# Two pairs of squared tiles added on GpSimd before TensorE's norm sum, at the first two FFN entries

## The chip, the cores and the metric

The kernel runs on one core of a Trainium2 chip. The metric is the device time of one execution in microseconds (us). Engines: PE is TensorE's matmul, PEld its weight load, DVE is VectorE, ACT is ScalarE, POOL is GpSimd, SP is SyncE, which here issues transfers (DMAs).

## The reference, cut to what matters

An encoder step of two layers runs over 576 tokens (512 of a prompt and 64 of a stream), each a row of 1024 numbers in float32. Every layer has two SwiGLU FFNs around a mixer, each behind an RMS norm, so there are four FFNs in all (a, b, c and d in the kernel).

```python
def _rmsnorm(x, g):
    x32 = x.astype(jnp.float32)
    y = x32 * lax.rsqrt(jnp.mean(x32 * x32, axis=-1, keepdims=True) + EPS) * g.astype(jnp.float32)
    return y.astype(x.dtype)

def _swiglu(u, w_in, w_out):
    h = u @ w_in
    a, b = h[..., :D_FF], h[..., D_FF:]
    return (jax.nn.silu(a) * b) @ w_out
...
        x = x + 0.5 * _swiglu(_rmsnorm(x, norm_ffn1[i]), ffn1_w_in[i], ffn1_w_out[i])
```

The part at issue is the mean over the 1024 channels of x squared, for each token, at the entry of the first FFN (a) and of the second (b).

## The kernel before, in words

The activations x lie in on-chip memory with the channel on the partition: 8 tiles (j = 0 to 7) of 128 channels by 576 tokens. Two neighbouring tiles make a block kp (0 to 3). Tokens are worked in two halves of 288.

**The matmuls.** Every product is in float32 accuracy by three matmuls on a split of both operands into a high part (copied by ACT) and a low part (subtracted by DVE). For the weights, ACT copies `w_hi` (L715) and DVE subtracts `w_lo` (L1213). The input product of an FFN takes, for each pair n of hidden tiles, seven block products M1 to M7 in place of eight (Strassen's way, in Winograd's form). The moving operand is one of seven combinations of the x blocks, held in `u7`: parts 0 and 1 are single blocks and simple differences, part 2 holds the last three sums (`sums_odd`, L1255 to L1259, three DVE operations that depend on each other; the high part is copied by ACT at L757, the low part subtracted by DVE at L1267). The weights are summed likewise: SP loads raw blocks (raw_x, raw_y, raw_a), DVE adds raw_y and raw_x into raw_z (L1219), and GpSimd issues accumulating transfers onto raw_x, raw_y and raw_z (`add_s1` L569, `add_s3` L577, `add_s4` L584).

**The order of the work** is written out by hand for each engine, and every engine goes through its own list in order; semaphores tie the lists together. A ring of weight places and the reuse of the raw buffers set how early a copy or a transfer may go: SP's load of M4's weights for pair n (`load_a22`, L449) waits until `w_lo` of M4 of the pair before is made, and what SP has behind it waits with it. At a and b the products of the first pairs come in the order COLD: M1 of pairs 0 and 1, M5, M2, then M6 of pairs 0 and 1 together, block by block (kp = 0 to 3), then M7, M7, M4, M3, M1 of pair 2, M5 of pair 2, M4 of pair 1, M6 of pair 2 and so on. Each kp of the M6 group waits for `u7_made[2]`, part 2 of u of that block. M5 of pair 2 waits for `gate_second` of pair 0 (DVE, L1314), and M6 of pair 2 for ACT's copy of M1 of pair 2 (`s1_copied`, L793).

**The norm.** The products use x without its norm; the factor `rstd` of each token is applied afterwards by DVE. At a and b ACT squares each tile of x into `sq8` (`square_tile`, L761), and PE sums over the channels by a matmul of `sq8` with a matrix filled with 1/1024 (`norm_tiles`, L1867 to L1876; the matmul is L1874), two halves for each tile, accumulated over the 8 tiles. In a, 2 tiles come ahead of the M6 group and 2, 1, 1 and 2 behind its four kp steps; in b, 4 come within the first M1 group and one behind each kp step of M6. Then ACT takes the root (L766) and DVE the reciprocal in four parts (L1284). At the other norms GpSimd squares and adds tile by tile (`square`, L540 to L556: L548 squares, L551 adds).

**GpSimd's list** at the entry of a or b (`add_rest`, L586): add_s1 of pair 2, add_s4 of pair 0, add_s4 of pair 1, add_s1 of pair 3 (which waits for SP's load into raw_x), then add_s3, add_s4 and add_s1 in turn.

Of the kernel before, what the change touches and what calls it, by code (L numbers as in the profile page):

```python
# [5 lines left out]
DT = D_MODEL // P  # L6
KP = DT // 2
SEQ, DEC_SEQ = 512, 64
TOK = SEQ + DEC_SEQ
HALF = TOK // 2  # L10
# [124 lines left out]
def encoder_step(nc, a):  # L135
    F32, F32R = mybir.dt.float32, mybir.dt.float32r
    ALU, ACT = mybir.AluOpType, mybir.ActivationFunctionType
# [10 lines left out]
    def sb(name, shape, dt=F32, at=None):  # L148
        size = 4
        for s in shape[1:]:  # L150
            size *= s
        return nc.alloc_sbuf_tensor_at(name, shape, dt, offset=region(size) if at is None else at)
# [43 lines left out]
    mean_w = sb("mean_w", [P, P])  # L196
# [50 lines left out]
    sq8 = sb("sq8", [P, DT, TOK], at=sq8_at)  # L247
# [6 lines left out]
    ps = nc.alloc_psum_tensor("ps", [P, 8, 512], F32)  # L254
# [25 lines left out]
    sem = nc.alloc_semaphore  # L280
# [16 lines left out]
    sums_made = [sem("sums_even_made"), sem("sums_odd_made")]  # L297
# [5 lines left out]
    h_hi_ready, h_ready = sem("h_hi_ready"), sem("h_ready")  # L303
    sq_step, sumsq_ready = sem("sq_step"), sem("sumsq_ready")
    sq_last, sumsq_full, sq8_made = sem("sq_last"), sem("sumsq_full"), sem("sq8_made")
    mix_squared, mix_added = sem("mix_squared"), sem("mix_added")
    hist_psum, hist_root, hist_rms = sem("hist_psum"), sem("hist_root"), sem("hist_rms")
    norm_psum, norm_root, rstd_ready = sem("norm_psum"), sem("norm_root"), sem("rstd_ready")
# [13 lines left out]
    ffn_a = Ffn(0, 0, a["ffn1_in"][0], a["ffn1_out"][0])  # L322
    ffn_b = Ffn(1, 2, a["ffn2_in"][0], a["ffn2_out"][0])
# [89 lines left out]
    with block as block:  # L413
# [111 lines left out]
        def _(pool):  # L525
# [39 lines left out]
            def add_s1(f, ph, n):  # L565

                g = f.pair(ph, n)
                pool.wait_ge(a21_landed[g % 2], 16 * (g // 2 + 1))
                pool.dma_start(raw_x[g % 2][:, :], f.w_in[ph * PAIRS + n, 3, :, :], accum_op=ALU.add) \  # L569
                    .then_inc(s1_summed[g % 2], 16)  # L570
# [9 lines left out]
            def add_s4(f, ph, n):  # L580

                g = f.pair(ph, n)
                pool.wait_ge(lo_split, f.unit(ph, "M6", n) + 1)
                pool.dma_start(raw_z[g % 2][:, :], f.w_in[ph * PAIRS + n, 1, :, :], accum_op=ALU.add) \  # L584
                    .then_inc(s4_summed[g % 2], 16)

            def add_rest(f, ph):

                if order_of(f.i, ph) is COLD:
                    add_s1(f, ph, 2)  # L590
                    add_s4(f, ph, 0)
                else:
                    add_s4(f, ph, 0)
                    add_s1(f, ph, 2)
                add_s4(f, ph, 1)
                add_s1(f, ph, 3)
                for n in range(2, PAIRS):
                    add_s3(f, ph, n)
                    add_s4(f, ph, n)
                    if n + 2 < PAIRS:  # L600
                        add_s1(f, ph, n + 2)
# [67 lines left out]
        def _(act):  # L669
# [78 lines left out]
            def u7_high(f, kp, part):  # L748

                if part == 1:  # L750
                    act.activation(u7[:, kp, 0, 2:4, :], halves(x[:, 2 * kp + 1, :]), ACT.Copy,
                                   scale=ngains[:, f.norm, 2 * kp + 1:2 * kp + 2]).then_inc(u7_hi[1], 1)
                    return
                act.wait_ge(sums_made[part // 2], KP * f.i + kp + 1)
                first, end = PARTS[part]
                src = stage(f, kp)[:, first:end, :] if part else even_stage(f, kp)
                act.activation(u7[:, kp, 0, first:end, :], src, ACT.Copy) \  # L757
                    .then_inc(u7_hi[part], 1)

            def square_tile(j):  # L760
                act.activation(sq8[:, j, :], x[:, j, :], ACT.Square).then_inc(sq8_made, 1)  # L761
# [160 lines left out]
            u7_high(ffn_a, 2, 2)  # L922
            square_tile(1)
            square_tile(3)
            u7_high(ffn_a, 3, 2)
            square_tile(5)
            square_tile(7)
            ffn_in(ffn_a, 0, copied=2)
            ffn_out(ffn_a, 0)
            ffn_in(ffn_a, 1)  # L930
# [138 lines left out]
            for j in range(DT):  # L1069
# [5 lines left out]
                elif middle:  # L1075
# [3 lines left out]
                    for h in range(HEADS):  # L1079
                        last = act.activation(junk[0:L, :], v_one[0:L, c, h, 0:DV], ACT.Square,  # L1080
                                              accum_out=ssum[0:L, c, h:h + 1])
# [727 lines left out]
        def _(pe):  # L1809
# [55 lines left out]
                                   start=True, stop=True)  # L1865
                mm.then_inc(norm_psum, 1)

            def norm_tiles(f, turns):

                for i in turns:  # L1870
                    j = (0, 2, 4, 6, 1, 3, 5, 7)[i] if f is ffn_a else i
                    pe.wait_ge(sq8_made, DT * f.i + i + 1)
                    for h in range(2):
                        mm = pe.matmul(ps[:, 6 + h, 0:HALF], mean_w[:, :], sq8[:, j, h * HALF:(h + 1) * HALF],  # L1874
                                       start=i == 0, stop=i == DT - 1, skip_group_check=True)
                    if i == DT - 1:  # L1876
                        mm.then_inc(norm_psum, 1)

            def ffn_in(f, ph):
                order = order_of(f.i, ph)  # L1880
                groups = [order[t:t + 1] for t in range(len(order))]
                if order is COLD:
                    groups = [order[0:2], order[2:3], order[3:4], order[4:6], order[6:8]] + groups[8:]
                elif ph == 0:
                    groups = [order[0:4]] + groups[4:]
                needs = {"M1": 0, "M5": 0, "M2": 1, "M3": 1, "M6": 2, "M7": 2, "M4": 2}
                seen, t = set(), 0
                for products in groups:
                    if ph == 0 and t == ROOT_AT[f.i]:
                        if f is ffn_a:  # L1890
                            norm_tiles(f, range(2))
                        elif f is not ffn_b:
                            norm(f.norm)
                    t += len(products)
                    for prod, n in products:
                        product_waits(f, ph, prod, n)
                    part = needs[products[0][0]]
                    for kp in range(KP):
                        if ph == 0 and part not in seen:
                            pe.wait_ge(u7_made[part], KP * f.i + kp + 1)  # L1900
                        for prod, n in products:
                            product_mm(f, ph, prod, n, kp)
                        if order is COLD and products[0] == ("M6", 0):
                            norm_tiles(f, ((2, 3), (4,), (5,), (6, 7))[kp] if f is ffn_a else (4 + kp,))
                        elif f is ffn_b and ph == 0 and products[0] == ("M1", 0) and kp == 1:
                            pe.wait_ge(x_ready, 2 * DT + 6)
                            norm_tiles(f, range(4))
                    seen.add(part)

            def ffn_out(f, ph, tiles=DT):  # L1910
# [162 lines left out]
            for k in range(DT):  # L2073
# [4 lines left out]
                mm = block_mm(U_M + 1, k, u_tile(k), 2, k == 0, k == DT - 1)  # L2078
# [262 lines left out]
```

## Time and profile before

| | us |
|---|---|
| median of 3 runs | 1898.39 |
| lowest and highest | 1894.95, 1899.76 |
| the profiled execution, its whole time | 1898.26 |
| its span in the trace | 1896.5 |
| PE busy | 1872.6 (99%) |
| DVE busy | 1253.8 (66%) |
| ACT busy | 866.4 (46%) |
| GpSimd busy | 329.1 (17%) |

All rows are of one profiled execution, with times from the start of its span. A row of a timeline gives the start, the length, the engine, the line of the kernel, the operation, what it writes and reads, and in brackets the idle time of the engine before it with what ended it. Matmuls overlap, so the spacing of their starts tells their cost, not their length. An instruction of DVE or ACT starts some 0.09 us before the one ahead of it is shown to end.

### The profile page before, as it was taken

How to read it: one execution, taken by the hardware profiler on the slowest of the kernel's cores; microseconds unless marked ns; L12 is line 12 of the kernel's file. 1: busy time of each engine (PE TensorE's matmuls, PEld its weight loads, DVE VectorE, ACT ScalarE, POOL GpSimd, SP SyncE). 2: the span in 40 equal slices, each digit the busy share in tenths (PEclk: the TensorE clock that was granted, in tenths of full speed). 3: DMA queues.
4: the chain of work that ended last, by engine and by line, in shares of the span. 5: the costliest groups of instructions: out<-in, count | busy, mean ns of one | idle time of the engine just before them, and what ended most of it. 6: DMA issues, size and time to landing. Idle time of an engine off the chain costs nothing.

```text
span 1896.5 us, 34433 instructions
## 1 busy us (share of the span) xinstructions
PE 1872.6 (99%) x13850; PEld 1849.8 (98%) x13850; DVE 1253.8 (66%) x1998; ACT 866.4 (46%) x1516; POOL 329.1 (17%) x352
## 2 busy tenths in 40 slices
PE   8999999999999999999999999999999999999998
PEld 7999999998999999999999999999989999999998
DVE  8874487668874488678853886453446888448843
ACT  7652355346552355345532553232334665235532
POOL 2210122121220122132201221300010322012112
PEclk9999999999999999999999999999999999999999
DMA  8763576334763576347644763221113576357632
GB/s 213 163 153 92 133 168 140 106 91 91 160 145 108 122 165 148 110 98 170 145 131 101 172 138 101 84 101 67 57 45 107 116 174 143 105 121 167 129 94 79
DMA packets 116830, 234.71 MB, mean 124 GB/s; under 512 B 13184, under 2 KB 15248, under 8 KB 116672
## 3 DMA queue, kind: packets, MB, share of 16 engines
q1 hardware_dynamic: 77440, 160.59, 28.0%
q0 software_dynamic: 38208, 69.42, 22.3%
q8 instruction: 111, 1.82, 0.4%
q10 hardware_dynamic: 1024, 2.49, 0.4%
q14 instruction: 47, 0.39, 0.1%
HBM read 228.92 MB, written 3.53 MB: 123 GB/s over the span
## 4 chain that ended last, share of the span: by engine, by line
PE 90%; DVE 4%; ACT 2%; DMA 2%; issue 1%; POOL 0%; DVEq 0%; ACTq 0%; POOLq 0%
PE ps L1829 48%; PE ps L1819 39%; DVE w_lo L1213 1%; DMA raw_y<-in_ffn_in 1%; DVE u L1267 1%; PE ps L2143 1%; PE ps L2209 0%; DMA raw_z<-in_ffn_in 0%; ACT w_hi L715 0%; PE ps L2146 0%; PE ps L2011 0%; PE ps L2133 0%; DMA x<-in_x 0%; PE ps L2118 0%; DVE rstd L1284 0%
## 5 line engine op out<-in xcount | busy, mean ns | idle before, releaser
L1829 PE MATMUL ps<-u,w_hi 128*128 128x288 f32 x4928 | 990.7, 297 | 12.8 <-DVE w_lo L1213 5.1
L1829 PEld LDWEIGHTS ps<-u,w_hi 128*128 128x128 f32 x4928 | 793.3, 189 | 18.0 <-DVE w_lo L1213 10.9
L1829 PE MATMUL ps<-u,w_lo 128*128 128x288 f32 x2464 | 729.0, 296 | 0.0
L1829 PEld LDWEIGHTS ps<-u,w_lo 128*128 128x128 f32 x2464 | 463.5, 188 | 0.0
L1819 PE MATMUL ps<-h_hi,w_lo 128*128 128x288 f32 x1386 | 298.0, 296 | 0.0
L1819 PE MATMUL ps<-h_hi,w_hi 128*128 128x288 f32 x1386 | 297.9, 296 | 0.0
L1819 PE MATMUL ps<-h_lo,w_hi 128*128 128x288 f32 x1386 | 297.8, 296 | 0.0
L715 ACT ACTIVATE w_hi<-w_raw 128x768 fp32r<-128x768 f32 (+3 forms) x164 | 136.1, 837 | 322.1 <-PE ps L1819 258.0
L1213 DVE TENSOR_TENSOR w_lo<-w_raw,w_hi 128x768 fp32r<-128x768 f32 (+3 forms) x164 | 167.8, 1032 | 163.1 <-ACT w_hi L715 160.9
L1819 PEld LDWEIGHTS ps<-h_lo,w_hi 128*128 128x128 f32 x1386 | 223.0, 189 | 0.0
L1819 PEld LDWEIGHTS ps<-h_hi,w_lo 128*128 128x128 f32 x1386 | 222.9, 189 | 0.0
L1819 PEld LDWEIGHTS ps<-h_hi,w_hi 128*128 128x128 f32 x1386 | 222.8, 189 | 0.0
L577 POOL DMA_DIRECT2D raw_y<-in_ffn_in x88 | 75.9, 870 | 809.1 <-DVE raw_z L1219 800.8
L715 ACT ACTIVATE w_hi<-raw_y 128x512 fp32r<-128x512 f32 x176 | 109.8, 631 | 183.1 <-PE ps L1829 83.1
L715 ACT ACTIVATE w_hi<-raw_z 128x512 fp32r<-128x512 f32 x176 | 110.9, 631 | 110.9 <-PE ps L1829 65.8
L1213 DVE TENSOR_TENSOR w_lo<-raw_z,w_hi 128x512 fp32r<-128x512 f32 x176 | 121.2, 689 | 53.6 <-ACT w_hi L715 52.9
L1213 DVE TENSOR_TENSOR w_lo<-raw_y,w_hi 128x512 fp32r<-128x512 f32 x176 | 122.8, 700 | 41.8 <-ACT w_hi L715 36.0
L1213 DVE TENSOR_TENSOR w_lo<-raw_a,w_hi 128x512 fp32r<-128x512 f32 x132 | 90.9, 688 | 37.8 <-ACT w_hi L715 37.8
L1819 PE MATMUL ps<-um_hi,w_hi 128*128 128x288 f32 x512 | 113.8, 304 | 0.6 <-DVE q_t L1566 0.4
L569 POOL DMA_DIRECT2D raw_x<-in_ffn_in x88 | 93.0, 1056 | 99.2 <-DMA raw_x<-in_ffn_in 97.7
L1819 PE MATMUL ps<-um_hi,w_lo 128*128 128x288 f32 x512 | 109.7, 296 | 0.0
L1819 PE MATMUL ps<-um_lo,w_hi 128*128 128x288 f32 x512 | 109.4, 295 | 0.0
(263 smaller groups left out, 2120.2 us busy)
## 6 DMA issues: line engine op xcount, KB each, us to landing
raw_a<-in_ffn_in SPq DMA_DIRECT2D x132, 256.0 KB, 3.8
w_raw<-in_ffn_out SPq DMA_DIRECT2D x64, 384.0 KB, 3.1
raw_y<-in_ffn_in SPq DMA_DIRECT2D x88, 256.0 KB, 3.5
raw_x<-in_ffn_in SPq DMA_DIRECT2D x88, 256.0 KB, 2.7
raw_x<-in_ffn_in POOLq DMA_DIRECT2D x88, 256.0 KB, 6.3
raw_y<-in_ffn_in POOLq DMA_DIRECT2D x88, 256.0 KB, 4.9
raw_z<-in_ffn_in POOLq DMA_DIRECT2D x88, 256.0 KB, 5.0
w_raw<-in_ffn_out SPq DMA_DIRECT2D x64, 320.0 KB, 3.1
```

The lines of the kernel that those rows point to most:

```text
L569: pool.dma_start(raw_x[g % 2][:, :], f.w_in[ph * PAIRS + n, 3, :, :], accum_op=ALU.add) \
L577: pool.dma_start(raw_y[g % 2][:, :], f.w_in[ph * PAIRS + n, 2, :, :], accum_op=ALU.add) \
L715: act.activation(w_hi[:, PLACE[u]:PLACE[u] + cols], src, ACT.Copy).then_inc(hi_split, 1)
L1213: dve.tensor_tensor(w_lo[:, PLACE[u]:PLACE[u] + cols], src, f32(w_hi[:, PLACE[u]:PLACE[u] + cols]), ALU.subtract).then_inc(lo_split, 1)
L1267: dve.tensor_tensor(u7[:, kp, 1, first:end, :], src, f32(u7[:, kp, 0, first:end, :]), ALU.subtract).then_inc(u7_made[part], 1)
L1819: mm = pe.matmul(ps[:, bank + h, 0:HALF], w, m[:, h * HALF:(h + 1) * HALF], start=first and p == 0, stop=last and p == 2)
L1829: mm = pe.matmul(dst, w, m, start=prod in ("M1", "M2", "M5") and kp == 0 and p == 0, stop=kp == KP - 1 and p == 2, skip_group_check=prod i ...
L2143: mm = pe.matmul(ps[0:L, 4 + h, 0:DV + 1], probs[0:L, h, c0:c0 + L], v_one[0:L, c, h, :], start=True, stop=c == 0)
```

## The change

GpSimd adds tile 6 to tile 4 and tile 7 to tile 5 of `sq8` at FFN a, and tile 5 to tile 4 and tile 7 to tile 6 at FFN b. The adds stand in GpSimd's list behind add_s4 of pair 1 and ahead of add_s1 of pair 3. Each waits for its squares and for sums of u: in a the first for those of block 2, the second for those of block 3; in b both for those of block 3. PE sums six tiles: in a 0 and 2 ahead of the M6 group, then 4, 1 and 3 behind kp = 1, and 5 behind kp = 3; in b 0 to 3 as before, 4 behind kp = 1 and 6 behind kp = 3. In a, ACT squares tiles 5 and 7 before it copies the high part of part 2 of u for block 3, and not behind it.

```diff
+            def add_squares(f, into, tile, made, sums):
+
+                pool.wait_ge(sq8_made, DT * f.i + made)
+                pool.wait_ge(sums_made[1], KP * f.i + sums)
+                pool.tensor_tensor(sq8[:, into, :], sq8[:, into, :], sq8[:, tile, :], ALU.add).then_inc(sq8_added, 1)
+
             def add_rest(f, ph):
...
                 add_s4(f, ph, 1)
+                if ph == 0 and f is ffn_a:
+                    add_squares(f, 4, 6, 4, 3)
+                    add_squares(f, 5, 7, DT, KP)
+                elif ph == 0 and f is ffn_b:
+                    add_squares(f, 4, 5, 6, KP)
+                    add_squares(f, 6, 7, DT, KP)
                 add_s1(f, ph, 3)
...
             square_tile(3)
-            u7_high(ffn_a, 3, 2)
             square_tile(5)
             square_tile(7)
+            u7_high(ffn_a, 3, 2)
...
-            def norm_tiles(f, turns):
-
-                for i in turns:
-                    j = (0, 2, 4, 6, 1, 3, 5, 7)[i] if f is ffn_a else i
-                    pe.wait_ge(sq8_made, DT * f.i + i + 1)
-                    for h in range(2):
-                        mm = pe.matmul(ps[:, 6 + h, 0:HALF], mean_w[:, :], sq8[:, j, h * HALF:(h + 1) * HALF],
-                                       start=i == 0, stop=i == DT - 1, skip_group_check=True)
-                    if i == DT - 1:
-                        mm.then_inc(norm_psum, 1)
+            def norm_tile(f, j, made=0, added=0, last=False):
+
+                if made:
+                    pe.wait_ge(sq8_made, DT * f.i + made)
+                else:
+                    pe.wait_ge(sq8_added, 2 * f.i + added)
+                for h in range(2):
+                    mm = pe.matmul(ps[:, 6 + h, 0:HALF], mean_w[:, :], sq8[:, j, h * HALF:(h + 1) * HALF],
+                                   start=made == 1, stop=last, skip_group_check=True)
+                if last:
+                    mm.then_inc(norm_psum, 1)
+
+            def norm_inside(f, kp):
+
+                if f is ffn_a and kp == 1:
+                    norm_tile(f, 4, added=1)
+                    norm_tile(f, 1, made=5)
+                    norm_tile(f, 3, made=6)
+                elif f is ffn_a and kp == 3:
+                    norm_tile(f, 5, added=2, last=True)
+                elif f is ffn_b and kp == 1:
+                    norm_tile(f, 4, added=1)
+                elif f is ffn_b and kp == 3:
+                    norm_tile(f, 6, added=2, last=True)
...
-                            norm_tiles(f, range(2))
+                            norm_tile(f, 0, made=1)
+                            norm_tile(f, 2, made=2)
...
                         if order is COLD and products[0] == ("M6", 0):
-                            norm_tiles(f, ((2, 3), (4,), (5,), (6, 7))[kp] if f is ffn_a else (4 + kp,))
+                            norm_inside(f, kp)
                         elif f is ffn_b and ph == 0 and products[0] == ("M1", 0) and kp == 1:
                             pe.wait_ge(x_ready, 2 * DT + 6)
-                            norm_tiles(f, range(4))
+                            for i in range(4):
+                                norm_tile(f, i, made=i + 1)
```

## Rows read from the trace of the kernel before

**Rows 1.** The page: busy time by engine, and the ended-last chain by engine

```profile
PE 1872.6 (99%) x13850; PEld 1849.8 (98%) x13850; DVE 1253.8 (66%) x1998; ACT 866.4 (46%) x1516; POOL 329.1 (17%) x352
...
PE 90%; DVE 4%; ACT 2%; DMA 2%; issue 1%; POOL 0%; DVEq 0%; ACTq 0%; POOLq 0%
```

**Rows 2.** Grouped lines: busy us, mean ns of one | idle us before

```profile
L551 POOL TENSOR_TENSOR sumsq<-sumsq,sq 128x576 f32<-128x576 f32 x26 | 37.7, 1452 | 2.0
...
L1874 PE MATMUL ps<-sq,mean_w 128*128 128x288 f32 x64 | 17.1, 406 | 0.0
```

**Rows 3.** Timeline of PE at the entry of FFN a (start, us, engine, line)

```profile
31.76 1.13 PE L1874 MATMUL ps<-sq,mean_w 128*128 128x288 f32 x4
32.52 0.64 PE L1829 MATMUL ps<-u,w_hi 128*128 128x288 f32 x2
...
33.13 0.43 PE L1829 MATMUL ps<-u,w_hi 128*128 128x288 f32 x2
...
44.10 0.51 PE L1829 MATMUL ps<-u,w_hi 128*128 128x288 f32 x2 [0.52 <-DVE tmp L1314]
...
47.88 0.51 PE L1829 MATMUL ps<-u,w_hi 128*128 128x288 f32 x2 [0.37 <-ACT side L793]
```

**Rows 4.** Timeline of DVE at the entry of FFN a

```profile
25.62 0.52 DVE L1259 SCALAR_TENSOR_TENSOR stage<-x,gains,stage 128x288 f32<-128x288 f32 x1
26.05 1.05 DVE L1267 TENSOR_TENSOR u<-stage,u 128x864 fp32r<-128x864 f32 x1
27.02 1.29 DVE L1213 TENSOR_TENSOR w_lo<-raw_y,w_hi 128x512 fp32r<-128x512 f32 x2
...
29.76 2.13 DVE L1267 TENSOR_TENSOR u<-stage,u 128x864 fp32r<-128x864 f32 x2
32.80 0.69 DVE L1213 TENSOR_TENSOR w_lo<-raw_a,w_hi 128x512 fp32r<-128x512 f32 x1 [0.90 <-ACT w_hi L715]
```

**Rows 5.** Timeline of ACT at the entry of FFN a

```profile
29.88 0.93 ACT L757 ACTIVATE u<-stage 128x864 fp32r<-128x864 f32 x1 [1.31 <-DVE stage L1259]
30.71 1.25 ACT L761 ACTIVATE sq<-x 128x576 f32<-128x576 f32 x2
```

**Rows 6.** Timelines of GpSimd and DVE near 834 and 1850 us

```profile
833.90 1.53 POOL L551 TENSOR_TENSOR sumsq<-sumsq,sq 128x576 f32<-128x576 f32 x1
...
834.06 1.92 DVE L1213 TENSOR_TENSOR w_lo<-raw_y,w_hi 128x512 fp32r<-128x512 f32 x1
...
1850.47 0.82 DVE L1213 TENSOR_TENSOR w_lo<-w_raw,w_hi 128x640 fp32r<-128x640 f32 x1
1850.47 1.83 POOL L548 TENSOR_TENSOR sq<-x 128x576 f32<-128x576 f32 x1 [5.47 <-DVE x L1795]
```

**Rows 7.** The ended-last chain in order of time: start us, us, what

```profile
33.52 4.12 DMA raw_a<-in_ffn_in
...
456.20 6.24 issue
...
463.51 7.46 DMA raw_y<-in_ffn_in
```

**Rows 8.** Timelines of DVE and PE at the entry of FFN b

```profile
456.89 1.05 DVE L1267 TENSOR_TENSOR u<-side,u 128x864 fp32r<-128x864 f32 x1
...
459.34 0.69 DVE L1213 TENSOR_TENSOR w_lo<-raw_z,w_hi 128x512 fp32r<-128x512 f32 x1 [0.81 <-ACT w_hi L715]
...
461.92 0.69 DVE L1213 TENSOR_TENSOR w_lo<-raw_x,w_hi 128x512 fp32r<-128x512 f32 x1 [0.55 <-ACT w_hi L715]
...
460.15 0.64 PE L1829 MATMUL ps<-u,w_hi 128*128 128x288 f32 x2
...
472.86 0.82 PE L1829 MATMUL ps<-u,w_hi 128*128 128x288 f32 x2 [2.57 <-DVE tmp L1314]
```

**Rows 9.** Stretches of time: busy us by engine, PE clock, DMA share, GB/s

```profile
456.00:472.00 16.00, 14.29 (x95) 13.21 (x93) 11.29 (x18) 8.62 (x17) 3.60 (x5) 1.00 0.93 218
472.00:476.00 4.00, 3.14 (x13) 3.17 (x14) 3.87 (x6) 1.91 (x3) 0.00 (x0) 0.57 0.55 119
```

More of the change, by code:

```diff
@@ L305, in encoder_step @@
     sq_last, sumsq_full, sq8_made = sem("sq_last"), sem("sumsq_full"), sem("sq8_made")
+    sq8_added = sem("sq8_added")
     mix_squared, mix_added = sem("mix_squared"), sem("mix_added")
```

## The prediction

> **What bounds the kernel now.** I read the page first: PE (TensorE) is busy 99% of the span and carries 90% of the chain that ended last [rows 1]. So a microsecond of TensorE work is worth a microsecond, but only in stretches where PE waits for nothing. The grouped lines give the size of what is at stake: 64 matmul records of the norm's sum, and a GpSimd add of a 128x576 tile, 1.45 us in the mean [rows 2]. Then I read the timelines of the two stretches that the diff touches, around 24 to 48 us (entry of the first FFN, a) and 440 to 476 us (entry of the second, b), to see what PE waits for there. In both, PE stands still a little later: at 44.10 for 0.52 us and at 47.88 for 0.37 us in a [rows 3], and at 472.86 for 2.57 us in b [rows 8]. Work that PE saves ahead of such a stop only makes the stop longer, unless what ends the stop comes earlier too. The chain view says what that is. In a: the load of raw_a (weights of product M4 of pair 1) issued at 33.52, landing 4.12 us later [rows 7], which SP issues only when DVE has made w_lo of M4 of pair 0, at 32.80 [rows 4]. In b: GpSimd's accumulating transfer into raw_y (M7 of pair 2), issued at 463.51, 7.46 us long [rows 7]. So a is set by DVE, ACT and a transfer, b by transfers, neither by the sum's matmuls.
>
> **TensorE's saving.** One tile of the sum is four records. The matmul behind it starts 0.76 us later, and its group then takes 0.64 instead of 0.43 us [rows 3]: 0.76 + 0.21 = 0.97 us for a tile. Two tiles fewer at each of two entries: 4 x 0.97 = 3.9 us. That is the whole of the prize, 0.2% of the time, under the 0.3% (5.7 us) that a measurement of this kernel can tell from no change. It counts in full only if PE's later stops shrink with it.
>
> **Entry a, step by step.** The diff puts ACT's squares 5 and 7 (1.25 us for the two) ahead of the high part of the last third of u for block 3. That copy waited for DVE until 29.88 with ACT idle 1.31 us [rows 5]: the two squares fit into that idle time, and all that ACT does behind 30.71 comes about 1.2 us sooner. This costs nothing; its cover is that idle time. DVE's idle 0.90 us before 32.80, which waited for ACT [rows 4], goes away: taken alone, DVE and the load of raw_a come 0.9 to 1.0 us earlier, and PE's restarts at 44.10 and 47.88 with them: a saving of 1.0 us, not 1.94, in a.
>
> Against this stand the two adds. Does a GpSimd add hold up DVE? At 834.06 DVE's subtraction of 128x512, 0.69 us at 32.80 [rows 4], lasted 1.92 us: it began just behind an add of GpSimd (833.90 to 835.43) and ended 0.55 us behind it. At 1850.47 GpSimd came second: its square of 1.15 us lasted 1.83, behind a DVE operation of 0.82 us [rows 6]. So whoever is second stands until the first is done. The Trainium skill (SBUF — State Buffer, "Who interferes with whom") says the same of DVE instructions with two SBUF inputs, and that the second one is blocked fully; charged as the full mean of 1.45 us for each add, the sum for a would be 0.4 us higher than mine.
>
> Add 1 may start at 26.14, the end of the sums of block 2 (25.62 + 0.52). DVE's u of block 1 has just started (26.05, 1.05 us) [rows 4], so the add waits to 27.0 and runs to 28.4; the DVE operation due at 27.02 stands, and DVE is 1.25 us late. The sums of block 3 end at 31.1; before, ACT had them at 29.88 [rows 5]. Add 2 waits for just that. DVE is by then in u of block 2 (until 32.1); the add runs to 33.4, and u of block 3 ends at 34.4, where it ended at 31.89 (29.76 + 2.13) [rows 4]. DVE is 2.5 us late. The idle 0.90 us and ACT's lead absorb about 1.0 of it: w_lo of M4 starts at 34.3, not 32.80: 1.5 us late. SP's load of raw_a waits for it, and two more SP loads stand in the queue behind that wait: all three go 1.5 us later; GpSimd's own next entry (add_s1 of pair 3) then goes at 33.5 at the earliest; its product M5 of pair 3 comes only behind the restart at 47.88, which is its cover. DVE's run from there to PE's restart is almost unbroken, so the restarts at 44.10 and 47.88 move by 1.5 us. PE itself waits at block 2 until 32.1 and at block 3 until 34.4, does the last sum tile behind that, and what it saves goes into the later stop. Entry a: **+1.5 us**. Bounds: -1.0 (the adds hold nobody up) and +1.9 (a full hold for each add).
>
> **Entry b.** There is no reordering here. Add 1 (tiles 4, 5) can run from 456.2, where GpSimd's issues ended [rows 7]; DVE's u of block 2 holds it to 456.9, where the next one started, it ends at 458.3. u of block 3 (456.89) ends 1.3 us late at 459.2, add 2 runs to 460.5, and w_lo of M4, next on DVE, is 2.5 us late. DVE idles 0.81 us before 459.34 and 0.55 us before 461.92 [rows 8], so w_lo of M5 of pair 2 is only 1.0 us late, and the accumulation into raw_y is issued at 464.5. PE waits for add 1 until 458.3 but has two sum tiles less between the blocks, so it starts block 3 at 460.1, as before (460.15 [rows 8]). What follows hangs on transfers: their engines are 93% busy from 456 to 472 us [rows 9], GpSimd waited 6.24 us there for its queue's next transfer [rows 7], and the one into raw_y lands close behind the transfer issued before it. An issue 1.0 us later is mostly hidden by that queue. Nearest rows give bounds of 0 and +1.0; I take **+0.5 us**, the middle. PE's savings, and the last sum tile, lie before the stop at 472.86 and buy nothing.
>
> **Sum.** +1.5 + 0.5 = +2.0 us. The profiled execution took 1898.26 us, its span 1896.5, so 1900.3 us; the median shown, 1898.39, is the same within 0.13 us. Behind 48 us and 476 us PE is again the bound, so the shifts pass to the end one to one.
>
> **Rivals.**
> 1. *The adds do not meet DVE, or DVE's delay is hidden.* For it: both adds wait for the sums, which spares the six longest dependent operations. Against it: DVE runs without a gap through the times of both adds in a, its first idle time being the 0.90 us before 32.80 [rows 4]. Then a gives -1.0 and b 0: 1897.3 us.
> 2. *The full saving.* PE's later stops move with it: -3.9, 1894.4 us. It needs raw_a 1.9 us earlier and raw_y 1.9 us earlier; nothing in the change speeds the transfers.
> 3. *Slower, by transfers and clock in b.* w_lo of M4 at 2.5 us late shifts three SP loads of 256 KB into the time when GpSimd's two accumulations run. At 218 GB/s [rows 9] each takes 1.2 us; if all three go ahead of raw_y it lands 3.6 us later, not 0.5. PE's stop is then 6 us long, and the granted clock, which fell to the 1.2 GHz level behind the 2.57 us stop (mean 0.57 over 472 to 476) [rows 9], stays there as long again: 3.14 us of work at 0.57 instead of 1 is 1.4 us lost once more. Sum: 1.5 + 3.6 + 1.4 = +6.5, 1904.8 us. It decides from raw_y landing 4 us later than now. Against it: SP's queue is still busy with the load of raw_x until 462.4, so the three would hardly start sooner anyway.
> 4. *Clock in a.* PE now waits 1 to 1.5 us twice within 30 to 35 us. If the clock falls there as in b, +1.4: 1901.7 us.
>
> **How the numbers follow.** Chances: forecast 0.55, rival 1 0.22, rival 2 0.05, rival 3 0.05, rival 4 0.13. Only rival 3 and some scatter are slower by over 0.3% (0.05); rival 2 with scatter can be faster by over 0.3% (0.02); the rest, 0.93, is within. The forecast alone holds 1898.5 to 1902. The range takes in rivals 1 and 4 and the scatter of the runs shown (1894.95 to 1899.76): 1896 to 1903.5 us; predicted 1900.3.
>
> **What would show it.** 48 sum records where there were 64. DVE operations of about 1.9 to 2.3 us where 0.7 to 1.05 stood, at about 27 and 32 to 34 us, and at 457 to 461. The chain view in a should still run over raw_a, issued near 35.0, and PE should restart near 45.6 and 49.4 instead of 44.10 and 47.88; in b its restart, counted from b's start, should come 0 to 1 us late. I am wrong if DVE's operations beside the adds keep their length, if raw_a is issued before 33.5, or if raw_y in b lands early enough to shorten the 2.57 us stop.

## The result, and the profile after

| | before | after |
|---|---|---|
| median of 20 runs each, us | 1898.93 (1894.95 to 1902.49) | 1902.24 (1897.75 to 1903.69) |
| profiled execution, us | 1898.26 | 1902.27 |
| its span, us | 1896.5 | 1900.5 |

The ratio of the times is 1.0014, its 95% interval 1.0007 to 1.0020: the change costs 2.7 us, between 1.3 and 3.8. (The two medians differ by 3.3 us; differences between kernels are given here by the ratio, which has an interval.) That is clear of no change, but under the 0.3%, 5.7 us, that the prediction took as the least that can be told apart. The forecast was +2.0 us and 1900.3 us, range 1896.0 to 1903.5; the time lies in it, 1.9 us above the forecast. Of those 1.9 us, 0.7 is that the forecast was added to one execution of 1898.26 us, where 20 runs have a median of 1898.93. In the later comparisons two executions, one of each kernel, took over 3000 us at a granted clock of 0.68 and 0.56; the ratios leave them out.

The page of the changed kernel: busy time by engine, the chain that ended last, and two of the grouped lines (busy us, mean ns of one | idle us before, and what ended it).

```profile
PE 1875.8 (99%) x13834; PEld 1852.9 (97%) x13834; DVE 1258.5 (66%) x1998; ACT 866.9 (46%) x1516; POOL 338.1 (18%) x356
...
PE 92%; DVE 5%; ACT 2%; DMA 1%; issue 1%; POOL 0%; DVEq 0%; ACTq 0%
...
L592 POOL TENSOR_TENSOR sq<-sq 128x576 f32<-128x576 f32 x4 | 9.3, 2338 | 3.1 <-DVE stage L1272 3.1
L1888 PE MATMUL ps<-sq,mean_w 128*128 128x288 f32 x48 | 13.1, 417 | 2.6 <-POOL sq L592 2.6
```

PE has 16 records fewer than in [rows 1], and the sum has 48 records, 13.1 us, where [rows 2] has 64 and 17.1 us. So the work did go away. Behind it stands what it cost: PE waits 2.6 us for the adds, and one add lasts 2338 ns in the mean, where the other adds of this shape last 1452 [rows 2].

**Entry a.** Timelines of DVE, GpSimd, SP's queue and PE of the changed kernel, 26 to 50 us.

```profile
26.15 0.52 DVE L1272 SCALAR_TENSOR_TENSOR stage<-x,gains,stage 128x288 f32<-128x288 f32 x1
...
27.55 2.52 DVE L1226 TENSOR_TENSOR w_lo<-raw_y,w_hi 128x512 fp32r<-128x512 f32 x2
...
31.53 3.25 DVE L1280 TENSOR_TENSOR u<-stage,u 128x864 fp32r<-128x864 f32 x2
34.71 0.68 DVE L1226 TENSOR_TENSOR w_lo<-raw_a,w_hi 128x512 fp32r<-128x512 f32 x1
```

```profile
26.82 2.10 POOL L592 TENSOR_TENSOR sq<-sq 128x576 f32<-128x576 f32 x1 [0.25 <-DVE stage L1272]
31.76 2.11 POOL L592 TENSOR_TENSOR sq<-sq 128x576 f32<-128x576 f32 x1 [2.83 <-DVE stage L1272]
```

```profile
35.41 0.33 SPq L450 DMA_DIRECT2D raw_a<-in_ffn_in  x1
```

```profile
45.76 0.51 PE L1842 MATMUL ps<-u,w_hi 128*128 128x288 f32 x2 [0.94 <-DVE tmp L1327]
49.54 0.51 PE L1842 MATMUL ps<-u,w_hi 128*128 128x288 f32 x2 [0.37 <-ACT side L806]
```

Read against [rows 4], the two subtractions behind add 1 take 2.52 us instead of 1.29, and the two products behind add 2 take 3.25 instead of 2.13. That is 1.23 + 1.12 = 2.35 us of standing still. The 0.90 us for which DVE waited ahead of w_lo<-raw_a are gone. The sums of block 2 already start 0.53 us later here than in the profile of before (26.15 against 25.62), ahead of anything that the change touches. With that taken off, PE's two restarts [rows 3] come 1.13 us late (45.76 - 44.10 - 0.53, and the same for 49.54).

**Entry b.** Timelines of DVE, GpSimd and PE, 456 to 477 us.

```profile
456.65 1.05 DVE L1280 TENSOR_TENSOR u<-spare,u 128x864 fp32r<-128x864 f32 x1
457.62 1.05 DVE L1280 TENSOR_TENSOR u<-side,u 128x864 fp32r<-128x864 f32 x1
458.59 1.89 DVE L1226 TENSOR_TENSOR w_lo<-raw_a,w_hi 128x512 fp32r<-128x512 f32 x1
460.41 1.89 DVE L1226 TENSOR_TENSOR w_lo<-raw_z,w_hi 128x512 fp32r<-128x512 f32 x1
```

```profile
456.64 5.11 POOL L592 TENSOR_TENSOR sq<-sq 128x576 f32<-128x576 f32 x2
...
466.16 0.85 POOL L578 DMA_DIRECT2D raw_y<-in_ffn_in  x1 [1.97 <-DVE raw_z L1232]
```

```profile
459.99 1.42 PE L1888 MATMUL ps<-sq,mean_w 128*128 128x288 f32 x4 [2.42 <-POOL sq L592]
...
461.93 0.68 PE L1842 MATMUL ps<-u,w_hi 128*128 128x288 f32 x2
...
465.57 0.42 PE L1842 MATMUL ps<-u,w_hi 128*128 128x288 f32 x2
...
476.88 0.50 PE L1842 MATMUL ps<-u,w_hi 128*128 128x288 f32 x2 [0.34 <-ACT side L806]
```

Four things are to be seen. Add 1 starts in the record at 456.64, but DVE's u of block 2 *and* its u of block 3 run at full length; only then does the add get its turn, and it ends at 459.95. PE waits 2.42 us for it. Then two PE records of the same kind take 0.68 us at 461.93 and 0.42 at 465.57: behind its wait PE ran for a while at the 1.2 GHz level. And the stop of 2.57 us of [rows 8] is gone: the only stop left near it is the 0.34 us at 476.88.

### The profile page after: what moved, and what is told of

It reads as the page before. It is cut to its first block, busy times and chain, and to the rows that moved or that the text cites. A ratio compares the mean times of both kernels' runs of the same rounds, so it can differ in the third digit from the quotient of the medians.

```text
span 1900.5 us, 34409 instructions
## 1 busy us (share of the span) xinstructions
PE 1875.8 (99%) x13834; PEld 1852.9 (97%) x13834; DVE 1258.5 (66%) x1998; ACT 866.9 (46%) x1516; POOL 338.1 (18%) x356
## 4 chain that ended last, share of the span: by engine, by line
PE 92%; DVE 5%; ACT 2%; DMA 1%; issue 1%; POOL 0%; DVEq 0%; ACTq 0%
PE ps L1842 49%; PE ps L1832 39%; DVE w_lo L1226 1%; DVE u L1280 1%; PE ps L2172 1%; PE ps L2238 0%; DVE rstd L1297 0%; PE ps L2175 0%; PE ps L2040 0%; PE ps L2162 0%; DMA x<-in_x 0%; PE ps L2136 0%; ACT w_hi L728 0%; DMA raw_y<-in_ffn_in 0%; PE ps L2147 0%
```

## What lies between two profiles of one kernel

The two profiles differ by 4.0 us, more than the 2.7 of the ratio, and all of it arises behind both entries. Stretches of the kernel before, of the same kernel again (experiment 7) and of the changed kernel; the columns are those of [rows 9].

```profile
1300.00:1316.00 16.00, 16.00 (x100) 13.60 (x101) 4.09 (x6) 5.11 (x7) 0.00 (x0) 1.00 0.10 34
```

```profile
1300.00:1316.00 16.00, 16.00 (x70) 12.80 (x70) 2.24 (x4) 3.01 (x4) 0.00 (x0) 0.68 0.10 34
```

```profile
1300.00:1316.00 16.00, 16.00 (x70) 13.25 (x70) 2.24 (x4) 3.01 (x4) 0.00 (x0) 0.68 0.10 33
```

PE never waits in these 16 us, but in the second and third the granted clock is 0.68 in the mean, and PE gets through 70 records instead of 100. At 16/100 = 0.16 us each, 30 records fewer are 4.8 us (an estimate from these rows). The unchanged kernel has this stretch too in its second profile: it does not need the change. Up to there the two profiles of before and after are level: PE's last stop ahead of it, a wait for DVE's `q_t`, ends at 1254.06 us before and at 1253.97 after. The first profile of before happened to be without it. The 13 later profiles, whatever the kernel, all show such a stretch there, of this length or shorter (a granted clock of 0.74 to 0.91 in the mean from 1298 to 1318 us).

So I compare two short stretches, each between two rows that every kernel has. **A** goes from the start of the sums of block 2 in FFN a (the DVE row at 25.62 of [rows 4]) to PE's second restart (47.88 in [rows 3]; in "six tiles, no adds" PE doesn't stop there, so the number is the start of the same pass). **B** goes from DVE's last `side<-x` of block 1 of FFN b (453.07 before) to ACT's next `side<-ps` ahead of PE's last restart (476.10 before).

| kernel | A, us | B, us | raw_y lands behind B's start, us |
|---|---|---|---|
| before | 47.88 - 25.62 = 22.26 | 476.10 - 453.07 = 23.03 | 17.90 |
| before, again | 48.60 - 26.80 = 21.80 | 476.38 - 453.45 = 22.93 | 17.79 |
| b only | 47.55 - 25.64 = 21.91 | 474.16 - 451.90 = 22.26 | 17.12 |
| 8 passes more | 47.84 - 26.08 = 21.76 | 473.14 - 452.67 = 20.47 | 15.34 |
| 24 passes more | 48.69 - 26.88 = 21.81 | 477.07 - 453.51 = 23.56 | 18.43 |
| 24 passes more, again | 47.78 - 26.02 = 21.76 | 474.36 - 452.53 = 21.83 | 16.69 |
| reordering | 47.44 - 25.84 = 21.60 | 473.03 - 452.19 = 20.84 | 15.70 |
| reordering, again | 47.36 - 25.78 = 21.58 | 474.14 - 451.88 = 22.26 | 17.12 |
| six tiles, no adds | 49.48 - 26.38 = 23.10 | 475.86 - 453.59 = 22.27 | 17.14 |
| adds only | 50.92 - 26.40 = 24.52 | 478.55 - 455.67 = 22.88 | 17.74 |
| writes for adds | 48.13 - 26.79 = 21.34 | 475.21 - 452.44 = 22.77 | 17.64 |
| a only | 50.48 - 26.58 = 23.90 | 476.54 - 455.35 = 21.19 | 16.05 |
| after | 49.54 - 26.15 = 23.39 | 476.35 - 453.81 = 22.54 | 16.55 |
| after, again | 50.01 - 26.75 = 23.26 | 476.88 - 454.33 = 22.55 | no wait for it |

A is sharp. The six profiles unchanged at a lie within 21.76 to 22.26, mean 21.88; the three with the whole change there lie at 23.39, 23.26 and 23.90, mean 23.52. **The change costs 1.6 us in A** (1.4 without "a only", where the clock fell in A as well). Most of it is still there 400 us later: from A's start to B's start the six take 426.68 us in the mean, the three 428.00, which is 1.3 us more (0.9 without "a only"). B strays: the eight profiles unchanged at b give 20.47 to 23.56, mean 22.01, and each is the landing of raw_y plus 5.13 or 5.14 us. The three with the whole change there give 22.26 to 22.55, mean 22.45: +0.4 us, but the mean of eight values that stray by 3 us is itself good to no better than some 0.5 us.

## The experiments

**1. The reordering alone** (run twice). ACT's squares 5 and 7 go ahead of the high part of u of block 3; nothing else.

```diff
             square_tile(3)
-            u7_high(ffn_a, 3, 2)
             square_tile(5)
             square_tile(7)
+            u7_high(ffn_a, 3, 2)
```

> Only the reordering on ScalarE at FFN a: squares 5 and 7 ahead of the high part of u of block 3; eight tiles on PE, no adds. Theory 1 (GpSimd's adds block VectorE, which sets the chain at a): without adds VectorE keeps its operations' length, w_lo of M4 comes 0.9 us earlier relative to the sums of block 2, and PE's restarts at M5 and M6 of pair 2 come 0.9 to 1.0 us earlier: total -1 us, ratio 0.9995. Rival (the adds cost nothing, the loss comes from the order): restarts as late as with the whole change, 1.1 us later than before. Theory 2, on the rest: the whole change's +2.7 us is mostly stretches at the 1.2 GHz level elsewhere, which depend on when the program passes; then this kernel's total may differ from before by 1 to 3 us either way although FFN a is 1 us faster.

> The same text as the reordering alone, once more, to tell how far an execution of one and the same kernel strays. Theory: in entry a the timeline repeats (DVE's idle time in front of the low part of M4 gone, M4's load issued near 32 us after the span's start, 1 us less between the sums of block 2 and the point behind both restarts), and the total is 0 to 1 us below the kernel before. Rival (the gain in a was a chance of the first profile): the segment in a is as long as before.

Measured: 1898.99 us, ratio 1.0002 (0.9993 to 1.0011); again 1900.30 us, 1.0003 (0.9994 to 1.0013). DVE and the chain in the second of them:

```profile
31.97 0.68 DVE L1213 TENSOR_TENSOR w_lo<-raw_a,w_hi 128x512 fp32r<-128x512 f32 x1
```

```profile
32.69 0.33 SPq L449 DMA_DIRECT2D raw_a<-in_ffn_in  x1
```

```profile
33.85 1.94 PE ps L1874 x8
35.79 1.62 PE ps L1829 x12
```

DVE's idle 0.90 us is gone, and counted from A's start raw_a is issued 1.0 us sooner (32.69 - 25.78 = 6.91 against 33.52 - 25.62 = 7.90), as expected. But A is 21.59 us against a mean of 21.88 unchanged: 0.3 us won (0.7 against the first profile of before alone), not 1.0, and the totals show no gain. The chain has moved off raw_a to PE itself, which sums eight tiles until 35.79. The chain in the repeat of the kernel before shows a third path of nearly the same length, through ACT:

```profile
36.43 0.47 ACT L766
...
37.73 0.74 ACT rstd L766
...
39.04 1.90 DVE w_lo L1213 x3
```

Here the load of raw_a is not in the chain at all. Three paths (raw_a, ACT's squares and rstd, PE's sum) end within some tenths of a microsecond of each other; relieving one gives what the next one leaves.

**2. Six tiles, no adds.** The order of PE and ACT is that of the change, but GpSimd adds nothing: two tiles are left out of each of the two norms. Against the changed kernel:

```diff
             def add_squares(f, into, tile, made, sums):
-                pool.wait_ge(sq8_made, DT * f.i + made)
...
+                return
```

> The whole change without GpSimd's adds: TensorE sums six squared tiles and two of the eight are left out of the norm at FFN a and b (that part of the sum is not computed). Theory 1: no blocking, VectorE's w_lo and u operations keep 0.69 and 1.05 us, a's restarts come 1.0 us earlier than before, b's wait for the tile behind kp 1 (2.42 us with the adds) disappears; b's restart is earlier by at most 0.7 us. Total -1 to -1.7 us, not the -3.9 us of four tiles. Rival (PE's time is all that counts): -3.9 us.

Measured: 1901.32 us, ratio 1.0007 (0.9997 to 1.0017), +1.3 us where -1.0 to -1.7 was expected: a miss, though the interval starts at -0.6. PE's stops, and stretches of time (clock last but two):

```profile
44.66 0.82 PE L1840 MATMUL ps<-u,w_hi 128*128 128x288 f32 x2 [1.97 <-DVE tmp L1325]
...
472.61 0.82 PE L1840 MATMUL ps<-u,w_hi 128*128 128x288 f32 x2 [3.17 <-DVE tmp L1325]
```

```profile
44.00:50.00 6.00, 5.33 (x28) 5.37 (x29) 4.90 (x8) 3.57 (x6) 0.00 (x0) 0.72 0.37 87
472.00:480.00 8.00, 7.39 (x37) 7.42 (x38) 6.87 (x12) 3.87 (x7) 0.85 (x1) 0.62 0.34 81
```

With four tiles less to sum and nobody blocked, the kernel is not measurably faster. What PE saved went into its next stops (1.97 us where the profile of before had 0.52 [rows 3], 3.17 where it had 2.57 [rows 8]), and behind each the clock was at the 1.2 GHz level for a time (0.72 and 0.62 in the mean). The first restart in a comes at 44.66 - 26.38 = 18.28 us behind A's start, 0.2 us sooner than before (44.10 - 25.62 = 18.48) and not the 1.0 expected: here the chain runs over `36.76 6.02 DMA raw_y<-in_ffn_in`, a GpSimd transfer. With the slower clock behind it, A comes out at 23.10 us, 1.2 longer than unchanged. So the whole prize of 3.9 us is not to be had by PE's savings alone, even with the adds free.

**3. The adds alone.** All eight tiles are summed and ACT keeps its old order. GpSimd does the four adds into a buffer that nobody reads; PE waits for none of them.

```diff
+                pool.tensor_tensor(sumsq[:, :], sq8[:, into, :], sq8[:, tile, :], ALU.add).then_inc(sq8_added, 1)
```

> The kernel before with GpSimd's four adds put in at the same places, into a tile nobody reads; ScalarE's order and TensorE's eight tiles as before. Theory 1: the adds alone make VectorE 2.3 to 2.5 us late at a; the idle 0.90 us before w_lo of M4 takes some of it; restarts at a 1.4 to 2.2 us later than before. At b VectorE's w_lo of M4 and M3 take 1.9 us each. Total +1.5 to +3 us. Rival (adds beside VectorE cost nothing): restarts where they were, total 0.

Measured: 1903.23 us, ratio 1.0021 (1.0012 to 1.0031), +4.0 us (2.3 to 5.9) where 1.5 to 3 was expected, the slowest of the change's parts. DVE beside the adds in a, and PE's restart:

```profile
27.80 2.51 DVE L1229 TENSOR_TENSOR w_lo<-raw_y,w_hi 128x512 fp32r<-128x512 f32 x2
...
34.81 1.20 DVE L1229 TENSOR_TENSOR w_lo<-raw_a,w_hi 128x512 fp32r<-128x512 f32 x1 [0.91 <-ACT w_hi L731]
```

```profile
47.14 0.50 PE L1847 MATMUL ps<-u,w_hi 128*128 128x288 f32 x2 [1.52 <-DVE tmp L1330]
```

A is 24.52 us, 2.6 more than unchanged, so the adds without the rest of the change cost more than the change's 1.6. Against the first profile of before it is 2.26 us (24.52 - 22.26), a little over the 1.4 to 2.2 expected, and the rows account for it: DVE stands 1.22 + 0.51 = 1.73 us, and the load of raw_a, `36.03 4.65 DMA raw_a<-in_ffn_in`, takes 0.53 us more than the 4.12 of [rows 7]. Add 2 held DVE for 0.51 us only, since in ACT's old order its squares come later and it fell mostly into DVE's idle 0.91 us. In the changed kernel the adds hold DVE for 2.35 us, but the idle time is gone.

**4. Writes in place of the adds.** Each add is two writes of a constant to the tile that it made, which read nothing; waits and order are those of the change. The norm is not the true one: two tiles are missing from each sum, and the two tiles that the adds should have made hold a constant. Against the changed kernel:

```diff
-                pool.tensor_tensor(sq8[:, into, :], sq8[:, into, :], sq8[:, tile, :], ALU.add).then_inc(sq8_added, 1)
+                pool.memset(sq8[:, into, :], 1.0).then_inc(set_step, 1)
+                pool.wait_ge(set_step, 2 * f.i + 1 + (into != 4))
+                pool.memset(sq8[:, into, :], 0.5).then_inc(sq8_added, 1)
```

> The whole change with each add replaced by two GpSimd memsets of the same tile (write only, nothing read; the sum of squares of these tiles is not computed). If GpSimd's reads are what stands in VectorE's way, as the Trainium skill says of VectorE operations with two SBUF inputs, VectorE's operations beside the memsets keep 0.69 and 1.05 us, and a's restarts come 0.9 to 1.0 us earlier than before. If any GpSimd operation does it, w_lo at about 27 us is stretched by the memset's length.

Measured: one run, 1901.46 us, so the total tells little. DVE and GpSimd:

```profile
28.19 1.29 DVE L1228 TENSOR_TENSOR w_lo<-raw_y,w_hi 128x512 fp32r<-128x512 f32 x2
...
30.93 2.13 DVE L1282 TENSOR_TENSOR u<-stage,u 128x864 fp32r<-128x864 f32 x2
```

```profile
27.43 0.58 POOL L592 MEMSET sq<- 128x576 f32 x1 [0.22 <-DVE stage L1274]
28.06 0.58 POOL L594 MEMSET sq<- 128x576 f32 x1
...
31.13 0.58 POOL L592 MEMSET sq<- 128x576 f32 x1 [2.49 <-DVE stage L1274]
31.77 0.58 POOL L594 MEMSET sq<- 128x576 f32 x1
```

DVE's operations keep the lengths of [rows 4] (1.29 and 2.13) beside GpSimd's writes. A is 21.34 us: 0.5 below the unchanged mean, 2.0 below the changed kernel's two (23.39 and 23.26). Only whether GpSimd reads the tiles, and how long it is at it (2 x 0.58 us against 1.42 for an add), differs between this and the change. So by this one profile the hold costs 2.0 us in A, and everything else in the change gives 0.5. The Trainium skill (SBUF — State Buffer, "Who interferes with whom") says that a DVE instruction with two SBUF inputs contends with a GpSimd instruction that reads SBUF and not with one that only writes it; this case's runs agree.

**5 and 6. The change at one entry only.** The diff of the change, cut to FFN a in one kernel and to FFN b in the other; the other entry sums its eight tiles as before.

```diff
                 if ph == 0 and f is ffn_a:
                     add_squares(f, 4, 6, 4, 3)
                     add_squares(f, 5, 7, DT, KP)
-                elif ph == 0 and f is ffn_b:
-                    add_squares(f, 4, 5, 6, KP)
-                    add_squares(f, 6, 7, DT, KP)
```

> The change at FFN a alone (reordering, two adds, six tiles), b as before. Theory 1: from the sums of block 2 to PE's restart at M6 of pair 2, 1.1 us longer than before; at b nothing of its own, so what b does there is the spread between executions. Total +1 us. If the loss seen in the whole change's median (+2.7 us) came mostly from b, this kernel would be within 0.5 us of before.

> The change at FFN b alone, a as before. Theory 1: GpSimd's first add at b loses the port to two VectorE operations in a row and takes 3.3 us, PE waits about 2.4 us for it behind kp 1, the accumulation into raw_y is issued 2 us later than before counted from b's start, but lands at nearly the same time: PE's restart at M6 of pair 2 between -0.5 and +1 us. Total 0 to +1 us. Rival: b costs +1.5 us or more, because the late issue shows in the landing.

Measured: a only 1901.90 us, ratio 1.0005 (0.9997 to 1.0014), +1.0 us; b only 1900.90 us, ratio 1.0003 (0.9994 to 1.0012), +0.6 us. Their sum, 1.6 us, fits the whole change's interval (1.3 to 3.8), but neither differs measurably from no change. So the expectation for "a only", which was to tell a's share from b's by 0.5 us, can't be decided by the totals. The stretches say more: A in "a only" is long, like after, and somewhat longer than expected (23.90 - 22.26 = 1.6 us, not 1.1), with the clock at 0.66 from 35 to 40 us. "b only" repeats the hold of the changed kernel in b:

```profile
454.74 1.05 DVE L1277 TENSOR_TENSOR u<-spare,u 128x864 fp32r<-128x864 f32 x1
...
456.68 1.89 DVE L1223 TENSOR_TENSOR w_lo<-raw_a,w_hi 128x512 fp32r<-128x512 f32 x1
```

Again the add, in the record from 454.73, is let through behind the second of the two products, and PE waits 2.42 us for it. But what follows differs from the changed kernel: PE's records behind the wait take 0.42 us, so the clock stayed at the 2.4 GHz level; the accumulation into raw_y was issued at 463.23 - 451.90 = 11.33 us behind B's start, 0.9 us later than in [rows 7] and not the 2 expected; and its landing again set PE's restart, as in the kernel before:

```profile
463.23 5.79 DMA raw_y<-in_ffn_in
```

```profile
470.91 0.50 PE L1839 MATMUL ps<-u,w_hi 128*128 128x288 f32 x2 [1.08 <-DVE tmp L1324]
```

**7 and 8. Both kernels again.** The texts of before and after, unchanged.

> The kernel before, unchanged, once more, for a second profile of it. Theory 2: the stretch at the 1.2 GHz level near 1300 us, which every profile but the first of before shows and which costs 4.7 us there, comes or stays away from one execution to the next of the same kernel; and PE's stop at b (2.57 us in the first profile) varies by 2 us with when raw_y lands. So this profile may show the stretch near 1300 us and a span of 1897 to 1902 us. Rival: the stretch near 1300 us never comes with the kernel before, so it is a consequence of the change.

> The changed kernel, unchanged, once more. Theory 1: the way from the sums of block 2 to PE's restart at M6 of pair 2 at a is again 1.1 us longer than before, within 0.3 us, since it is set by VectorE's list; b's restart and the stretch near 1300 us may differ from the first profile by 1 to 5 us. Total again 1 to 3 us over before.

Measured: before again 1899.90 us, ratio 0.9998 (0.9988 to 1.0007); after again 1901.94 us, ratio 1.0007 (0.9998 to 1.0017), +1.3 us. The two results for the changed kernel, +2.7 and +1.3, have intervals that overlap from 1.3 to 3.2 us. The second profile of before has the stretch near 1300 us, so the rival that only the changed kernel has it is refuted. A in the second profile of after is 23.26 us, 1.0 over the first profile of before, as expected.

**9 and 10. A known delay elsewhere** (10 is run twice). Matmul passes of M1 of pair 5 in the third FFN are done over, 8 times in one kernel and 24 in the other, where PE waits for nobody. The question: is a small delay measured at its size?

```diff
+                if (f.i, ph, prod, n, kp) == (2, 1, "M1", 5, 0):
+                    w, m = passes(u, kp, u7[:, kp, 0, piece, :], u7[:, kp, 1, piece, :])[0]
+                    for _ in range(24):
+                        pe.matmul(dst, w, m, start=True, stop=True)
```

> The kernel before with 8 matmul passes of 288 columns done over once in the third FFN, where TensorE is the bound: 0.13 us each, 1.05 us, and nothing else is altered. Theory (a delay in a stretch that TensorE bounds goes to the end one to one, and what is seen at the 1.2 GHz level near 1300 us belongs to the execution, not to the kernel): 1.0 us over the kernel before, and the stretch near 1300 us there or not regardless of the shift. Rival (a small shift decides whether the stretch occurs): this kernel differs from the next by clearly more or less than 2.1 us.

> The same with 24 passes done over, 3.15 us. Theory: 3.1 us over the kernel before, 2.1 over the kernel with 8, which also gives the size of difference that these runs can still see. Rival: the two differ by something else than 2.1 us because one of them has the long stretch at the 1.2 GHz level near 1300 us and the other has not.

> The same text with 24 passes done over, once more and in more rounds, since it came out 7 us over the kernel before where 3.1 was expected, on few executions. Theory (chance: the executions of one text stray by a few us, in stretches at the 1.2 GHz level and in landings): near 3.1 us this time, 1 to 5. Rival (the shift or the longer program brings something of its own): 6 to 8 us again.

Measured: 8 passes 1899.52 us, ratio 1.0009 (0.9999 to 1.0018), +1.7 us where 1.0 was expected. 24 passes 1905.31 us, ratio 1.0038 (1.0023 to 1.0053), +7.2 us on four runs, where 3.1 was expected: a miss, the interval excludes 3.1. The same text again, in 12 runs on another chip: 1903.75 us, ratio 1.0022 (1.0011 to 1.0033), +4.2 us, with 3.1 inside. The traces show what the totals can't. From the first of the passes to the end of PE's stop near 1254 us it is 1252.25 - 1085.20 = 167.05 us with 8 passes, 1261.30 - 1092.15 = 169.15 with 24, and 1255.40 - 1086.26 = 169.14 with 24 again: 2.1 us for 16 passes at 0.13. So the delay is passed on at its size, at least up to there. In the first profile with 24 passes the excess lies ahead of them: they start at 1092.15 us, 5.9 us later than the 1086.26 of the second, in two kernels with the same text. One comparison of a few runs can be wrong by some 4 us here, more than the whole change.

## Why the prediction was right, point by point

**TensorE's saving: right, and lost as said.** 48 records; 13.1 us for 17.1. Experiment 2 shows that it runs into PE's next stops; that the longer stops can also bring the 1.2 GHz level behind them was not in that part of the forecast.

**Entry a, +1.5 forecast, 1.6 measured in A.** Its parts: "DVE is 1.25 us late" behind add 1 measured 1.23; the hold by add 2, 1.25 by the same working, measured 1.12; the idle 0.90 us and ACT's lead, "about 1.0", took 0.97 (w_lo of M4 starts 34.71 - 32.80 - 0.53 = 1.38 us late where 2.35 were held); "raw_a issued near 35.0" was 35.41, less the 0.53 by which this profile was late already, 34.88. The restarts were put near 45.6 and 49.4. They came at 45.76 and 49.54, which looks exact, but less the same 0.53 it is 45.23 and 49.01: 1.13 us late, not 1.5, among other things because raw_a took 3.89 us and not 4.12. That a GpSimd add and a DVE operation with two inputs hold each other up was read from two rows [rows 6]; experiments 3 and 4 show it as the cause of DVE's delay. Bounds of -1.0 and +1.9 held.

One term was too large: "a saving of 1.0 us" for the reordering alone. DVE and raw_a did come 1.0 us earlier; the step that failed is "and PE's restarts ... with them". Experiment 1 gives 0.3, since ACT's and PE's paths lay right behind raw_a's. This did not spoil the sum, because in the full change the hold makes DVE and raw_a the last path again (the chain of waits runs over u, w_lo<-raw_a and `35.41 3.89 DMA raw_a<-in_ffn_in`). Against the profile of before, from which the forecast was made and which had A longest of the six, the cost reads 1.1; against their mean, 1.6. The forecast of 1.5 lies between; that it meets the second so closely is in part luck.

**Entry b, +0.5 forecast, 0.4 ± 0.5 measured: the size fits, the mechanism does not.** The step that failed is "DVE's u of block 2 holds it to 456.9 ..., it ends at 458.3", and with it "it starts block 3 at 460.1, as before". GpSimd lost to two DVE operations in a row, not to one, and add 1 ended 6.14 us behind B's start (459.95 - 453.81), not 5.2 (458.3 - 453.07). PE stood 2.42 us, and then in both profiles of the changed kernel the clock was at the 1.2 GHz level. Block 3, whose first pass was at 460.15 - 453.07 = 7.08 us behind B's start [rows 8], starts at 462.65 - 453.81 = 8.84: 1.8 us late. (In "b only", where the clock stayed up, it is 459.94 - 451.90 = 8.04, 1.0 us late; the rest is the clock.) The accumulation into raw_y is issued at 466.16 - 453.81 = 12.35 us behind it, where before it was 463.51 - 453.07 = 10.44: 1.9 us late, not 1.0 (1.6 in the second profile, 0.9 in "b only").

That this costs only 0.4 in the mean fits the reason that was given, that the late issue of raw_y is hidden in its landing. Issued 1.9 us later, it landed 4.2 us on, at 470.36 (ACT's w_hi<-raw_y, which waited for it, starts at 470.38), or 16.55 us behind B's start; unchanged, it landed at 15.3 to 18.4. With it came one of the prediction's own signs of being wrong, "if raw_y in b lands early enough to shorten the 2.57 us stop": that stop is gone. The chain of the changed kernel near 460 to 467 us shows what bounds b instead:

```profile
456.64 3.31 POOL sq L592
459.94 0.04 issue
459.99 1.42 PE ps L1888 x4
461.41 2.88 PE ps L1842 x12
464.29 1.05 PE ps L1888 x4
465.34 1.60 PE ps L1842 x12
```

So in both profiles of the changed kernel the wait for a transfer, which sometimes comes early (B 20.47) and sometimes late (23.56), became a wait for an add and PE's work at the slower clock behind it (B 22.54 and 22.55). In "b only" it did not: the clock stayed up, and raw_y, landing at 17.12, set B at 22.26, 5.14 us behind it as in every unchanged kernel. The later of the two paths counts. It follows, as an estimate and not as a measurement, that an execution whose raw_y would have landed early loses up to 2 us by the change (22.5 - 20.5), and one whose raw_y lands late loses nothing. That three profiles averaged +0.4 where +0.5 was forecast is luck.

**The rivals.** Rival 1 (the adds don't meet DVE) is refuted by the stretched rows. Rival 2 (full saving) is refuted by the result, and experiment 2 shows that even free adds gave no gain. Rival 3 (raw_y 4 us later) did not come: raw_y landed no later. Rival 4 (clock in a) came in one profile of three: "a only" has a clock of 0.66 in 35 to 40 us, the changed kernel 1.00 both times, behind waits of 0.48 and 1.15 us in its first profile. In b the 1.2 GHz level was forecast behind the stop at 472.86 if that grew; it came instead behind the wait for add 1 that ended at 459.99. That wait was in the forecast, but shorter (until 458.3) and with no word of the clock.

**The total.** 1.6 + 0.4 = 2.0 us by stretches, 2.7 (1.3 to 3.8) and 1.3 (-0.4 to 3.2) by the ratios. Nothing calls for a further effect, and nothing excludes one of a microsecond. That shifts pass to the end one to one is borne out in part, by A (1.3 of 1.6 us are left at B's start) and by the passes of experiments 9 and 10; in between, the kernels stray too much for a shift of 2 us to be followed (from B's start to PE's stop near 1254 us the kernel before takes 801.0 us in one profile and 802.1 in the other, and the two with 24 passes 807.8 and 802.9). No part of the change, alone, has a ratio below 1.

## What to carry to other kernels

Before handing work to GpSimd, look at what DVE does at that time: here an add that reads two tiles held back DVE's operations with two inputs for most of its own 1.42 us (1.12 to 1.23 us), and was itself held back by up to two of them in a row. Moving work off the busiest engine pays only where that engine has no stop behind the work; take it away without a substitute (experiment 2) to learn the most that it could bring. And before a difference of some 0.1% is put down to a change, profile the unchanged kernel twice: here one stretch of clock, present or not, was worth more than the change.

## What was not expected of the hardware

- An add of GpSimd whose record begins 0.01 us ahead of a DVE operation (456.64 and 456.65) still had to let that one and the next, back to back, go first: 3.31 us for an add of 1.42 (the length of the one at 34.04 in experiment 3). In all three profiles with the change at b it was so, and in experiment 3. In a, the add got its turn behind one DVE operation each time (2.10 us). What decides this wasn't tested.
- In b the DVE operations next in line took 1.89 us instead of 0.69 both times: they were held for 1.20 us by each add.
- Behind the same wait of 2.42 us at b the granted clock fell to the 1.2 GHz level in both profiles of the changed kernel (0.61 and 0.72 in the mean from 460 to 464 us) and stayed at 1.00 in "b only". It fell behind 2.57 us in the first profile of before (0.57 over 472 to 476) and stayed at 1.00 behind 2.50 us in the second. What decides it wasn't tested.
- The accumulating transfer into raw_y took 4.9 to 8.0 us from issue to landing in kernels that don't differ up to there (4.88 with 8 passes more, 7.98 with 24, both edited only behind it), and 4.2 in the changed kernel.
- One and the same kernel strays from execution to execution: the stretch near 1300 us at the 1.2 GHz level was missing once in 14 profiles of these kernels, was of different length in the others, and worth up to 4.8 us.
